# Seven-place expert ring: the down weights of two places loaded in three partition pieces instead of one

## The chip, the cores and the metric

One core of one Trainium2 chip runs the whole kernel. The metric is device time in microseconds (us) of that core. A profiled execution gives, beside its own time, a span from the first to the last instruction and a trace of engines and DMA packets. The engines are PE (matrix products), DVE (vector), ACT (scalar functions), POOL (GpSimd) and SP (which here issues the large DMAs). Sixteen DMA engines carry every transfer.

## The reference

One layer of a streaming encoder block on 256 tokens of width 1024, all in float32:

```python
h = rms_norm(x, norm_mix_gain)
proj = h @ w_in                       # q/k/v, gates, beta, decay: 5640 columns
y_a = diff_attention(...)             # 4 heads
y_b = gated_delta_net(...)            # 4 heads, chunks of 64
merged = sigmoid(m_gate_a) * (y_a @ w_branch_attn) + sigmoid(m_gate_b) * (y_b @ w_branch_gdn)
x = x + merged @ w_out
h2 = rms_norm(x, norm_ffn_gain)
x = x + hier_moe(h2, ...)             # 32 experts: 1024 -> 256 (gate, up) -> 1024 (down), 2 per token
out = rms_norm(x, norm_final_gain)
```

The change touches only how the down weights of the 32 experts (256 x 1024 float32 each, 1 MB) come from HBM to SBUF.

## The kernel before

The first 280 us are the projection, the two mixers, the output projection and the routing. The rest is the mixture of experts. Its 32 experts are visited in order, one unit of 32 token rows each (four units form a group). For every unit PE gathers the tokens of a group (line 1152), multiplies by gate and up weights (`hidden`, line 1194), turns the activation (line 1203), multiplies by the down weights (`down`, line 1239) and, once for every four units, scatters the result into the output (`scatter`, line 1249). `rolling` (line 1253) interleaves the steps: the gate and up product of unit u+1 stands ahead of the down product of unit u. The last units have forms of their own, `down_half` (line 1206) and `scatter_half` (line 1219).

Every expert needs three weights of 1 MB: gate, up and down. They live in seven places ("slots") of SBUF, of 24 KB per partition each; an eighth place holds gate and up alone, for expert 7. Expert e has its down weights in place e % 7 (`place`, line 60). A 1 MB weight is laid over 128 partitions, 8 KB of consecutive bytes in each.

All of these loads go out from SP, in program order, on one queue. `load_expert` (line 310) issues the first loads: experts 0 to 2 between the chunks of `w_in` in the first 50 us, expert 7's gate and up, and experts 3 to 6 between 234 and 266 us. From 280 us on, SP runs through the reloads: in step i it issues gate and up of expert 8+i (line 387, after a wait on `gateup_used`) and then down of expert 7+i into place i % 7 (line 392, after a wait on `experts_used`). The two waits say that PE and DVE are through with what the place held. The steps i = 0 to 22 are of this form, the first seven written out, the next fourteen in a hardware loop over two rounds of seven, the rest written out. Then come the missing columns of gate and up of expert 31 (line 412; six eighths of them were fetched early), down of expert 30, the down weights of expert 31 in two halves (line 418) and the final gain row (line 422).

A load adds 16 to its semaphore `down{slot}` when it has landed, and PE waits ahead of `down` until it stands at 16 times the number of loads that the place has had (lines 1209 and 1232).

```python
def reload_down(e, slot, used):
    sp.wait_ge(s["experts_used"], used)
    sp.dma_start(c.down_flat[slot], down_d[:, e, :].rearrange("p a f -> p (a f)")).then_inc(s[f"down{slot}"], 16)
```

Of the kernel before, what the change touches and what calls it, by code (L numbers as in the profile page):

```python
# [22 lines left out]
P = 128  # L23
# [17 lines left out]
SLOTS = 7  # L41
# [3 lines left out]
EXP_F = 3 * D * HID // P  # L45

EARLY = (4, 2)
BIG = 1e30
LAMBDA_INIT = 0.2

# [231 lines left out]
def sync_program(sp, c, io):  # L282

    s = c.s
# [11 lines left out]
    def load_chunk(i):  # L296
# [10 lines left out]
            sp.dma_start(dst[:, 0:k0, :], w_in[:, 0:k0, col:col + n]).then_inc(s["first_loaded"], 16)  # L307
        sp.dma_start(dst[:, k0:, :], w_in[:, k0:, col:col + n]).then_inc(s[f"stage_loaded{i % 2}"], 16)

    def load_expert(e):  # L310
        slot = e
        for flat, name, sem in ((c.gate_flat, "moe_w_gate", "gateup"), (c.up_flat, "moe_w_up", "gateup"),
                                (c.down_flat, "moe_w_down", "down")):
            if e == SLOTS and name == "moe_w_down":
                break
            k = 2 if name == "moe_w_down" else KD
            if e == SLOTS - 2:
                sp.wait_ge(s["mix_out"], 2)
            if e == SLOTS - 1:
                sp.wait_ge(s["mix_out"], 4)  # L320
            sp.dma_start(flat[slot], io[name][0, e].rearrange("(p k) f -> p (k f)", k=k)).then_inc(s[f"{sem}{slot}"], 16)

    load_chunk(0)
    load_chunk(1)
    load_expert(0)

    def row(dst, src, sem):
# [13 lines left out]
    for j in range(1, OWN):  # L341
        load_expert(j)
        load_chunk(2 + j)
    load_chunk(5)
    load_expert(SLOTS)
    for i in range(6, NCH):
        load_chunk(i)

    for j, name in enumerate(("w_branch_attn", "w_branch_gdn")):
        i = NCH + j  # L350
# [3 lines left out]
    for j in range(2):  # L354
        i = NCH + 2 + j
# [12 lines left out]
    def load_early(part, at, k0):  # L368

        for g, name in enumerate(("moe_w_gate", "moe_w_up")):  # L370
            sp.dma_start(at[:, g, :], io[name][0, EXPERTS - 1].rearrange("(p k) f -> p (k f)", k=KD)[:, k0 * HID:(k0 + part) * HID])\
                .then_inc(s["early_loaded"], 16)
    sp.wait_ge(s["logits_ready"], len(PIECES))
    load_early(EARLY[0], c.early_flat[0], 0)
    sp.wait_ge(s["x1_parked"], 1)
    sp.wait_ge(s["h2_ready"], NT)
    load_early(EARLY[1], c.early_flat[1], EARLY[0])

    gate_d = io["moe_w_gate"][0].rearrange("e (p k) f -> p e (k f)", k=KD)
    up_d = io["moe_w_up"][0].rearrange("e (p k) f -> p e (k f)", k=KD)  # L380
    down_d = io["moe_w_down"][0].rearrange("e (p k) d -> p e (k d)", k=2)
# [7 lines left out]
    def reload_down(e, slot, used):  # L389

        sp.wait_ge(s["experts_used"], used)
        sp.dma_start(c.down_flat[slot], down_d[:, e, :].rearrange("p a f -> p (a f)")).then_inc(s[f"down{slot}"], 16)

    def one(e):
        return slice(e, e + 1)
# [1 line left out]
    def reload_both(e, j, used, first=False):  # L397
        reload_gateup(e(1), j, used if first else used + 1)
        reload_down(e(0), j, used)
# [8 lines left out]

    e, i, had = EXPERTS - 1, loads - 1, sum(EARLY) * HID
    sp.wait_ge(s["gateup_used"], i + 2)  # L410
    for flat, src in ((c.gate_flat, gate_d), (c.up_flat, up_d)):
        sp.dma_start(flat[i % SLOTS][:, had:], src[:, one(e), had:].rearrange("p a f -> p (a f)")).then_inc(s[f"gateup{i % SLOTS}"], 16)
    reload_down(one(e - 1), i % SLOTS, i + 1)

    sp.wait_ge(s["experts_used"], e - SLOTS + 1)
# [356 lines left out]
def down_out(c, i, q):  # L772

    return c.ps[ROWS * q:ROWS * (q + 1), 2 + i % 2, 0:256]
# [7 lines left out]
def need(eng, sem, value, first):  # L782

    if not first or value > 0:
        eng.wait_ge(sem, value)
# [17 lines left out]
def tensor_program(pe, c, io):  # L803
    s = c.s
# [95 lines left out]
    i = CI["bdg"]  # L900
# [158 lines left out]
    for n in range(4):  # L1059
        j, half = n // 2, n % 2  # L1060
        i = NCH + j
# [99 lines left out]
    def windows(nwin):  # L1161
# [8 lines left out]
        def weights(slot, k, early):  # L1170

            if early and k < EARLY[0]:
                return c.early_w[0][:, :, k, :]
            if early and k < sum(EARLY):
                return c.early_w[1][:, :, k - EARLY[0], :]
            return c.gu_w[slot][:, :, k, :]
# [29 lines left out]
        def down_half(i, at, half):  # L1206

            slot, times = at[2:4]
            pe.wait_ge(s["last_down" if half else f"down{slot}"], 16 if half else times * 16)
            if half == 0:  # L1210
                pe.wait_ge(s["actT_ready"], EXPERTS)
                pe.wait_ge(s["out_copied"], 2 * EXPERTS - 4)
            for kk in range(2):
                for q in (2 * half, 2 * half + 1):
                    last = pe.matmul(down_out(c, i, q), c.actT[i % 2][:, kk * ROWS:(kk + 1) * ROWS], c.down_w[slot][:, kk, 256 * q:256 * (q + 1)],
                                     start=(kk == 0), stop=(kk == 1))
            last.then_inc(s["down_ready"], 1)
# [10 lines left out]
        def down(unit, i, at, fresh, first, last_expert=False):  # L1228

            slot, times = at[2:4]  # L1230
            if fresh:
                pe.wait_ge(s[f"down{slot}"], times * 16)
                if last_expert:
                    pe.wait_ge(s["last_down"], 16)
            pe.wait_ge(s["actT_ready"], unit + 1)
            need(pe, s["out_copied"], unit * 2 - 2, first)
            for kk in range(2):
                for q in range(4):
                    last = pe.matmul(down_out(c, i, q), c.actT[i % 2][:, kk * ROWS:(kk + 1) * ROWS], c.down_w[slot][:, kk, 256 * q:256 * (q + 1)],  # L1239
                                     start=(kk == 0), stop=(kk == 1))  # L1240
            last.then_inc(s["down_ready"], 1)
# [44 lines left out]
        def alone(grp, at, first, experts=()):  # L1286

            if not first:
                gather(grp)
            turn_weighted(grp, 1)  # L1290
            fresh = [i == 0 or at[i] != at[i - 1] for i in range(GROUP)]
            hidden(grp, 0, at[0], fresh[0], first)
            for i in range(GROUP):
                if i == 0:
                    pe.wait_ge(s["Se_ready"], grp + 1)
                if i < GROUP - 1:
                    hidden(grp, i + 1, at[i + 1], fresh[i + 1], first)
                turn_act(grp * GROUP + i, i)
                down(grp * GROUP + i, i, at[i], fresh[i], first, EXPERTS - 1 in experts[i:i + 1])
            scatter(grp)  # L1300
# [73 lines left out]
def vector_program(v, c, io):  # L1374
# [3 lines left out]
    def chain(ins):  # L1378
        n[0] += 1
        ins.then_inc(s["dve_chain"], 1)  # L1380

    def settle():
        v.wait_ge(s["dve_chain"], n[0])
# [7 lines left out]
    def side(name):  # L1391
        v.wait_ge(s["side_ready"], SI[name] + 1)
        return c.side[side_pair(name)]
# [235 lines left out]
    def maxima(qt):  # L1629

        nk = P * (qt + 1)
        for m in range(2):
            ps = side(f"s{qt}{m}").rearrange("p (h k) -> p h k", h=H)
            chain(v.memset(ps[0:CHUNK, :, nk - CHUNK:nk], -BIG))
            settle()
# [306 lines left out]
def route(v, c, chain, settle):  # L1942
# [15 lines left out]
    def over(ap, n):  # L1958
        return ap.rearrange("p (t a) -> p t a", a=1).to_broadcast([P, NT, n])

    def link(ins):
        chain(ins)
        settle()
# [16 lines left out]
    link(v.tensor_tensor(group, cand, over(c.first, GROUPS), ALU.is_equal))  # L1980
    link(v.tensor_scalar(outside, group, 1.0, BIG, ALU.subtract, ALU.mult))
    link(v.tensor_tensor(inside.rearrange("p t (g e) -> p t g e", g=GROUPS), lg[:, :, GROUPS:].rearrange("p t (g e) -> p t g e", g=GROUPS),
# [41 lines left out]
def build(nc, io):  # L2024
    with ExitStack() as ctx:
        c = lay_out(nc, ctx)

        c.A_stored = nc.dram_tensor("stored_A", (2 * H * (P * P + P),), F32, kind="Internal").ap()
        c.inverses_stored = nc.dram_tensor("stored_inverses", (2, 2 * H, P, BLOCK), F32, kind="Internal").ap()
        block = ctx.enter_context(nc.Block())  # L2030

        @block.sync
        def _(sp):
            sync_program(sp, c, io)

        @block.gpsimd
        def _(pool):
            gpsimd_program(pool, c, io)

        @block.scalar  # L2040
        def _(act):
            scalar_program(act, c, io)

        @block.tensor
        def _(pe):
            tensor_program(pe, c, io)

        @block.vector
        def _(v):
            vector_program(v, c, io)  # L2050
# [24 lines left out]
```

## Time and profile before

| | |
|---|---|
| median of 3 runs | 481.01 us (480.9 to 481.35) |
| profiled execution, its time | 480.55 us |
| its span | 478.8 us |
| PE busy | 443.7 us (93%) |
| DVE busy | 206.1 us (43%) |
| ACT busy | 123.5 us (26%) |
| bytes moved by DMA | 137.13 MB, 286 GB/s over the span |
| share of the span in the chain that ended last | PE 78%, DMA 12%, DVE 4% |

Some 1.75 us of the profiled execution lie outside its span. Busy shares are averages over stages with different limits: PE is busy at 93% in all, and has waits on DMA only in the last 80 us. In the views below, "DMA share" is the mean busy share of the 16 DMA engines in a stretch, and can read a little over 1 because packets of one engine overlap by some nanoseconds. PEclk is the granted clock of TensorE, 1.00 for full speed.

### The profile page before, as it was taken

What the parts mean: (1) busy time and instruction counts of PE and PEld (TensorE: products, weight loads), DVE (VectorE), ACT (ScalarE), POOL (GpSimd) and SP (SyncE); (2) the same over time, 40 slices, a digit from 0 to 9 for tenths busy, and PEclk for the clock granted to TensorE, in tenths of its full rate; (3) what the DMA queues carried; (4) which work ended last, traced back from release to release, by engine and by line L of the source; (5) the groups of instructions that cost most, each with busy time, mean ns of one, the idle gap of its engine ahead of it and who ended that gap; (6) DMA issues with size and microseconds to landing.
All of it is one profiled execution on the core that took longest, in us unless ns stands there. A gap on an engine that the chain in (4) does not pass through costs nothing.

```text
span 478.8 us, 10293 instructions
## 1 busy us (share of the span) xinstructions
PE 443.7 (93%) x4337; PEld 336.4 (70%) x4337; DVE 206.1 (43%) x588; ACT 123.5 (26%) x311; POOL 11.8 (2%) x36
## 2 busy tenths in 40 slices
PE   8999999999999999999999798998989896698793
PEld 7885698875988799888645487575767664566451
DVE  1366287997344451711310645343434342413324
ACT  5001523001032230420012643232323322212234
POOL 6011000000000000000000000000000000000000
PEclk9999999999999999999999999999999998978798
DMA  8969947717504050444399869999999999999972
GB/s 314 399 198 349 410 155 235 287 41 213 177 7 171 0 177 2 175 177 175 127 421 414 330 258 422 417 417 422 418 420 417 420 420 419 420 419 422 418 284 93
DMA packets 38178, 137.13 MB, mean 286 GB/s; under 512 B 8561, under 2 KB 9905, under 8 KB 26225
## 3 DMA queue, kind: packets, MB, share of 16 engines
q1 hardware_dynamic: 33776, 135.22, 71.4%
q10 hardware_dynamic: 4352, 1.21, 1.2%
q8 instruction: 36, 0.59, 0.5%
q14 instruction: 14, 0.11, 0.1%
HBM read 134.59 MB, written 1.84 MB: 285 GB/s over the span
## 4 chain that ended last, share of the span: by engine, by line
PE 78%; DMA 12%; DVE 4%; issue 2%; ACT 2%; ACTq 0%; DVEq 0%
PE ps L868 30%; PE ps L1194 11%; DMA arena<-in_moe_w_up 6%; PE ps L1090 6%; PE ps L1075 6%; DMA ring<-in_moe_w_up 6%; PE ps L1152 5%; PE ps L1239 4%; PE ps L1249 4%; PE ps L886 3%; PE ps L1203 2%; DMA cst_in<-in_norm_ffn_gain 1%; PE ps L1021 1%; PE ps L983 1%; PE ps L906 1%
## 5 line engine op out<-in xcount | busy, mean ns | idle before, releaser
L868 PE MATMUL ps<-arena 128*128 128x256 f32 (+1 forms) x640 | 155.9, 401 | 0.2 <-ACT arena L516 0.2
L868 PEld LDWEIGHTS ps<-arena 128*128 128x128 f32 x640 | 119.9, 190 | 29.0 <-issue 14.6
L1194 PE MATMUL ps<-arena 128*32 128x128 f32 x1072 | 40.8, 292 | 9.8 <-DMA arena<-in_moe_w_up 6.0
L1194 PEld LDWEIGHTS ps<-arena 128*32 128x32 f32 x1072 | 31.3, 114 | 17.8 <-issue 7.8
L1194 PE MATMUL ps<-ring,arena 128*32 128x128 f32 x912 | 34.4, 293 | 8.4 <-DMA ring<-in_moe_w_up 7.1
L681 ACT ACTIVATE gains<-ps 32x256 f32<-32x256 f32 x62 | 23.3, 376 | 56.9 <-PE ps L1239 56.6
L1194 PEld LDWEIGHTS ps<-ring,arena 128*32 128x32 f32 x912 | 26.6, 114 | 14.8 <-DMA ring<-in_moe_w_up 8.6
L1849 DVE TENSOR_TENSOR masks<-ps,masks 128x64 f32<-128x64 f32 x32 | 7.2, 224 | 62.9 <-ACT masks L662 62.7
L1152 PEld LDWEIGHTS ps<-masks,arena 128*128 128x128 f32 x256 | 29.4, 193 | 3.4 <-issue 3.4
L1152 PE MATMUL ps<-masks,arena 128*128 128x128 f32 x256 | 30.8, 279 | 0.8 <-DVE masks L1786 0.8
L1864 DVE COPY arena<-ps 32x256 f32<-32x256 f32 x62 | 25.8, 416 | 11.5 <-PE ps L1239 10.2
L1090 PE MATMUL ps<-arena 128*128 128x512 f32 x64 | 28.3, 595 | 0.0
L1075 PE MATMUL ps<-arena 128*128 128x256 f32 x128 | 28.0, 379 | 0.0
L1075 PEld LDWEIGHTS ps<-arena 128*128 128x128 f32 x128 | 24.2, 190 | 3.3
L1090 PEld LDWEIGHTS ps<-arena 128*128 128x128 f32 x64 | 11.9, 190 | 13.4 <-issue 13.4
L568 ACT ACTIVATE arena<-ps 128x1024 f32<-128x1024 f32 x7 | 7.2, 1023 | 51.9 <-PE ps L868 32.4
L668 ACT ACTIVATE masks<-ps 64x64 f32<-64x64 f32 x32 | 6.9, 217 | 41.4 <-PE ps L1203 41.4
L1239 PE MATMUL ps<-arena,masks 128*32 128x256 f32 x256 | 17.0, 382 | 0.0
L1203 PE MATMUL ps<-masks 128*64 128x128 f32 x128 | 15.1, 316 | 1.2 <-DVE masks L1851 1.0
L1249 PE MATMUL ps<-arena,rw 128*128 128x512 f32 x28 | 16.2, 660 | 0.0
L1239 PE MATMUL ps<-ring,masks 128*32 128x256 f32 x240 | 16.0, 382 | 0.0
L1834 DVE TENSOR_TENSOR arena<-ps,small 128x512 f32<-128x512 f32 x8 | 5.5, 692 | 23.4 <-PE ps L1152 23.4
(271 smaller groups left out, 465.7 us busy)
## 6 DMA issues: line engine op xcount, KB each, us to landing
arena<-in_w_in SPq DMA_DIRECT2D x9, 2048.0 KB, 9.1
arena<-in_moe_w_gate SPq DMA_DIRECT2D x16, 1024.0 KB, 23.4
arena<-in_moe_w_up SPq DMA_DIRECT2D x16, 1024.0 KB, 24.8
arena<-in_moe_w_down SPq DMA_DIRECT2D x16, 1024.0 KB, 23.6
ring<-in_moe_w_down SPq DMA_DIRECT2D x15, 1024.0 KB, 23.7
ring<-in_moe_w_gate SPq DMA_DIRECT2D x14, 1024.0 KB, 20.3
ring<-in_moe_w_up SPq DMA_DIRECT2D x14, 1024.0 KB, 22.6
arena<-in_w_out SPq DMA_DIRECT2D x2, 2048.0 KB, 8.2
```

The costliest lines, as they stand in the source:

```text
L568: act.activation(dst, c.pair[i % 2], func).then_inc(s[sem], 1)
L681: last = act.activation(stacked(c, i, q), down_out(c, i, q), ACT.Copy)
L868: last = pe.matmul(out, lhs, rhs, start=(k == 0 and (i > 0 or part % 2 == 0)), stop=(k == KD - 1), skip_group_check=(i == 0))
L886: last = pe.matmul(blk(ps, i), lhs(t, h), rhs(t, h), start=True, stop=True)
L1075: last = pe.matmul(blk(branch_out(c, half), b, TOK), w[:, k, (4 * half + b) * P:(4 * half + b + 1) * P], yT[:, k, :], start=(k == 0), stop ...
L1090: last = pe.matmul(c.ps[:, 4 + 2 * t + half, :], mg, w[:, k, :], start=(k == 0), stop=(k == KD - 1))
L1152: last = pe.matmul(gather_out(c, k), c.h2[:, t, k, :], c.oh[:, t, :], start=(t == 0), stop=(t == NT - 1))
L1194: last = pe.matmul(c.ps[ROWS * q:ROWS * (q + 1), i % 2, 0:P], c.Hg[:, k, ROWS * i:ROWS * (i + 1)], w[:, :, start:start + 127:2], start=(k ...
L1203: last = pe.matmul(c.ps[64 * half:64 * half + 64, i % 2, 0:P], c.act[i % 2][:, 0:64], c.ident, start=True, stop=True)
L1239: last = pe.matmul(down_out(c, i, q), c.actT[i % 2][:, kk * ROWS:(kk + 1) * ROWS], c.down_w[slot][:, kk, 256 * q:256 * (q + 1)], start=(kk ...
L1249: last = pe.matmul(y_out(c, half, t), c.S_e[:, t * P:(t + 1) * P], c.Y[half], start=False, stop=False, skip_group_check=True)
L1864: last = v.tensor_copy(stacked(c, i, q), down_out(c, i, q))
```

## The change

The places 2 and 5 are named in `PARTED`. Wherever a whole down weight is loaded into one of them, in `load_expert` and in `reload_down`, three DMAs are issued instead of one: partitions 0 to 111, partitions 112 to 119, and partitions 120 to 127. Each adds 16 to the same semaphore, so for these two places PE waits for 48 per load and not for 16. The bytes, the order of the loads, the waits of SP and all other places are as they were. The two half loads of expert 31 go to place 3 and are not touched. Nine loads are of the new form: experts 2 and 5 at first, and as reloads the experts 9, 12, 16, 19, 23, 26 and 30.

```diff
+PARTED = (2, 5)
+DOWN_SIGNALS = [48 if i in PARTED else 16 for i in range(SLOTS)]
...
+    def down_parts(slot):
+        return [slice(0, P - 16), slice(P - 16, P - 8), slice(P - 8, P)] if slot in PARTED else [slice(0, P)]
...
-            sp.dma_start(flat[slot], io[name][0, e].rearrange("(p k) f -> p (k f)", k=k)).then_inc(s[f"{sem}{slot}"], 16)
+            src = io[name][0, e].rearrange("(p k) f -> p (k f)", k=k)
+            for rows in down_parts(slot) if name == "moe_w_down" else [slice(0, P)]:
+                sp.dma_start(flat[slot][rows], src[rows]).then_inc(s[f"{sem}{slot}"], 16)
...
     def reload_down(e, slot, used):
 
         sp.wait_ge(s["experts_used"], used)
-        sp.dma_start(c.down_flat[slot], down_d[:, e, :].rearrange("p a f -> p (a f)")).then_inc(s[f"down{slot}"], 16)
+        for rows in down_parts(slot):
+            sp.dma_start(c.down_flat[slot][rows], down_d[rows, e, :].rearrange("p a f -> p (a f)")).then_inc(s[f"down{slot}"], 16)
...
-            pe.wait_ge(s["last_down" if half else f"down{slot}"], 16 if half else times * 16)
+            pe.wait_ge(s["last_down" if half else f"down{slot}"], 16 if half else times * DOWN_SIGNALS[slot])
...
-                pe.wait_ge(s[f"down{slot}"], times * 16)
+                pe.wait_ge(s[f"down{slot}"], times * DOWN_SIGNALS[slot])
```

## Rows read from the trace of the kernel before

**Rows 1.** The page's chain that ended last, shares of the span.

```profile
PE 78%; DMA 12%; DVE 4%; issue 2%; ACT 2%; ACTq 0%; DVEq 0%
```

**Rows 2.** Waits of PE, 280 to 479 us: total us, times, longest.

```profile
PE ps L1194 <- DMA ring<-in_moe_w_up: 7.1, 2, 3.8
PE ps L1194 <- DMA arena<-in_moe_w_up: 6.0, 2, 3.9
```

**Rows 3.** Timeline of PE, 395 to 455 us: start, us, what, [idle before <-releaser].

```profile
402.70 1.36 PE L1194 MATMUL ps<-ring,arena 128*32 128x128 f32 x32 [3.84 <-DMA ring<-in_moe_w_up]
...
418.63 1.94 PE L1194 MATMUL ps<-arena 128*32 128x128 f32 x32 [3.92 <-DMA arena<-in_moe_w_up]
...
448.89 1.94 PE L1194 MATMUL ps<-ring,arena 128*32 128x128 f32 x32 [3.26 <-DMA ring<-in_moe_w_up]
```

**Rows 4.** Windows: stretch, busy us of the engines, PEclk, DMA share, GB/s.

```profile
core 0: us, PE busy (x) PEld busy (x) DVE busy (x) ACT busy (x) POOL busy (x), PEclk, DMA share, GB/s
281.00:449.00 168.00, 148.30 (x2610) 106.34 (x2614) 63.78 (x203) 47.50 (x168) 0.00 (x0) 0.96 1.01 417
```

**Rows 5.** DMA queues, 281 to 449 us: packets, MB, share of 16 engines.

```profile
q1 hardware_dynamic: 9563, 69.69, 100.2%
q8 instruction: 21, 0.34, 0.8%
q14 instruction: 5, 0.04, 0.1%
```

**Rows 6.** Windows over the end of the last loads.

```profile
460.00:461.00 1.00, 1.00 (x37) 0.94 (x37) 0.00 (x0) 0.43 (x2) 0.00 (x0) 1.00 0.97 385
...
461.00:466.00 5.00, 3.93 (x100) 2.66 (x94) 1.72 (x6) 2.78 (x7) 0.00 (x0) 1.00 0.48 188
...
466.00:467.00 1.00, 1.00 (x20) 0.51 (x23) 0.00 (x0) 0.67 (x4) 0.00 (x0) 1.00 0.00 0
```

**Rows 7.** The last issues, by line: durations in ns, starts; time to landing.

```profile
L422 SPq DMA_DIRECT2D arena<-in_norm_final_gain x1: 4289/4289/4289, 449.2 to 449.2; - x1
...
DMA to landing us min/median/max: 17.2/17.2/17.2
```

**Rows 8.** The two half loads of expert 31, by line.

```profile
L418 SPq DMA_DIRECT2D arena<-in_moe_w_down x2: 2157/3401/4645, 442.3 to 444.5; - x2
...
DMA to landing us min/median/max: 20.6/21.1/21.6
```

**Rows 9.** Timeline of SP: first and last reloads of place 2.

```profile
295.84 0.33 SPq L392 DMA_DIRECT2D ring<-in_moe_w_down  x1
...
436.02 6.28 SPq L392 DMA_DIRECT2D ring<-in_moe_w_down  x1
```

**Rows 10.** Store from 32 partitions: its line, and the queues from 107 to 109 us.

```profile
L574 ACTq DMA_DIRECT2D stored_inverses<-arena x2: 312/378/444, 106.7 to 107.0; - x2
...
q10 hardware_dynamic: 96, 0.26, 57.2%
```

**Rows 11.** Store of the output from 128 partitions: the queues from 474.5 to 478.5 us.

```profile
q1 hardware_dynamic: 288, 1.05, 65.5%
```

**Rows 12.** Timeline of PE at the end.

```profile
465.89 1.07 PE L1239 MATMUL ps<-ring,masks 128*32 128x256 f32 x16
466.79 1.09 PE L1215 MATMUL ps<-arena,masks 128*32 128x256 f32 x16
```

## The prediction

> **What bounds the kernel now.** I read the chain that ended last first. It is 78% PE and 12% DMA [rows 1], so a change to loads can matter only where the DMA part lies. The list of PE's waits from 280 us on has four on a DMA, 7.1 + 6.0 = 13.1 us in all, and every one is the product with gate and up weights waiting for an up weight [rows 2]. The timeline shows where: three of the four stand at 402.70, 418.63 and 448.89 us [rows 3], the fourth lies between the last two. So PE has slack until some 400 us and is paced by the loads from there to 448.89. After that no wait on a DMA follows, and the remaining 29.9 us of the 478.8 us span are a fixed tail. **The end is the landing of that last awaited weight plus 29.9 us.**
>
> Which weight is it? Counting the expert products back from the end (31 at 462.5, 30 at 458.7), the one at 448.89 belongs to expert 29, and what it awaits is the up load of step i = 21. Before it stand 21 steps of three loads and one gate, 65 loads with itself. The windows show the stream without a hole: DMA share 1.01 and 417 GB/s over 168 us [rows 4]. At 16 engines and one packet of 8 KB per partition, the queue's row gives the price of a packet: 100.2% of 16 x 168 us over some 8,500 weight packets (69.69 MB / 8 KB) is 0.317 us [rows 5]. A load of 128 partitions is 8 packets per engine, 2.53 us.
>
> A load has landed when the last of the 16 engines is through. How far are they apart? At the end of the stream the share is 0.97 in the us before 461, 0.48 on average over 461 to 466, and 0 after [rows 6]; the gain row, last in the queue, lands at 449.2 + 17.2 = 466.4 [rows 7]. So the first engines are idle from about 461 and the last works to 466.4: some 5 us between the first and the last. In those 5.4 us the mean engine works 5 x 0.48 = 2.4 us, so it is through 3.0 us ahead of the last. One cause is visible: 21 instruction packets of 16 KB, at 0.8% x 16 x 168 us = 21.5 us or 1.0 us each [rows 5], which an engine carries beside its share of weights. Spread evenly they would be 1.3 us for each engine; a gap of 5 us needs some engines to carry most of them. No view names these engines.
>
> **The change, part by part.**
>
> *SP's issues.* Two more DMAs in each of 9 loads. A reload of place 2 takes SP 0.33 us early in the stream, and 6.28 us late in it, when SP is held up because the queue ahead is full [rows 9]. Loads issued 17 to 22 us ahead of their landing [rows 7, 8] hide an issue of 0.4 us. Cost 0; without this cover 2 x 0.4 x 6 = 5 us. The first loads of places 2 and 5 (about 44 and 250 us) lie where PE waits for no weight. Also 0. What is queued behind each on SP are the next gate and up, with the same cover.
>
> *PE's waits.* The same waits on another number. 0.
>
> *The 112-partition piece.* One packet less for each engine if 16 engines still carry it, seven each: -0.317 us per load on all of them.
>
> *The two pieces of 8 partitions.* The trace has no such load in the stream. One packet is one partition, so at most eight engines carry a piece; if nothing holds them up it costs each of them one packet, 0.317 us. At the other end the eight packets go one after the other, 8 x 0.317 = 2.5 us. What is nearest in the trace? A store of 2 x 128 KB that has 32 partitions at the SBUF end: 64 packets of 4 KB in 57.2% of 16 x 2 us, 0.286 us each [rows 10]. The output's store has packets of the same 4 KB from 128 partitions: 65.5% of 16 x 4 us over 256 of them, 0.164 us each [rows 11]. With four times fewer partitions under the same 16 engines a packet takes 1.74 times as long. So a few partitions can't be served at the rate of the engines: 32 gave 16 x 4,096 B / 0.286 us = 229 GB/s, 7.2 GB/s per partition. At this rate 8 partitions give 57 GB/s, and a piece of 64 KB takes 1.14 us. I take this value; the ends 0.317 and 2.5 us stay for the range.
>
> The Trainium skill states the rule behind it: in "SBUF — State Buffer", Door 1, four neighbouring partitions share one of 16 ports, and the rate of a DMA goes by the ports that its partitions reach. By its map each piece here reaches two ports and would take about 1.2 us, an estimate from its 27.2 GB/s per port; the trace agrees on the 32 partitions. The page "DMA: Bandwidth & Descriptors", on how many engines a DMA uses, would put 8 partitions on the eight lowest-numbered engines, both pieces on the same eight; no row here shows it.
>
> *The sum.* An engine that carries both pieces spends 7 x 0.317 + 2 x 1.14 = 4.50 us on a parted load instead of 2.53, +1.97 us. Ahead of the awaited up weight lie the steps with i % 7 = 2 or 5: 2, 5, 9, 12, 16, 19, six loads. That is +11.8 us. The engines are up to 5 us apart, so they don't always meet at the same partitions; I take nine tenths, +10.6 us. Against it stands the lead: an average engine is 3.0 us ahead of the one that ends a load now, and this much is swallowed. Net **+7.6 us** on the landing at 448.89, and, since only the fixed tail follows, on the end. The other eight engines gain 6 x 0.317 = 1.9 us, but are no longer last.
>
> The seventh parted reload (expert 30) comes after that landing. It adds 2.0 us to the loads behind it: the halves of expert 31, which land at about 463.9 and 465.1 [rows 8], would be at 465.9 and 467.1 in the old timing, while their first product starts at 466.79 [rows 12] and the second half is used about 0.5 us on. This is just covered; 0, at worst 0.5.
>
> Against its own time: 480.55 + 7.6 = 488.2 us for an execution like the profiled one; the median of the runs is 0.46 us above that, so 481.0 + 7.6 = **488.6 us**.
>
> **The rivals.**
>
> *A. The pieces don't queue, and they go to the engines with the lead.* Then each parted load moves one packet from the eight late engines to the eight early ones: 1.9 us less on the one side, 1.9 us more on the other, by the sixth. Even engines would be worth 3.0 us [rows 6]; the late ones can come down by 1.9 at most, and the latest of the early ones comes up by as much and takes over before that. I put it at -1.3 us: 479.7 us. For it: instruction packets are real, and 5 us apart is what they would leave on few engines. Against: rows 10. It decides the sign where a piece costs these engines less than about 0.43 us: twelve times the excess over 0.317 must stay under 1.3 us.
>
> *B. No queueing, but the eight are the late ones.* +6 x 0.317 = +1.9 us, 482.9 us. It hangs on which engines fetch instructions, which no view tells.
>
> *C. A little queueing that eats the gain of A*, within 0.9 us: 481.0 us. It needs a piece at 0.35 to 0.5 us.
>
> *D. The 112-partition piece queues too.* Seven partitions per engine no longer fall the way eight do; if two engines meet throughout at the price of rows 10, the piece costs 0.74 x 2.2 = 1.6 us more on every engine, 9.8 us over six loads, so about +17 us: 498 us. Against: the 128-partition loads and the 32-partition store both run at what their partitions allow, and 112 lies near 128.
>
> *E. The loads aren't what is awaited.* If PE had slack, nothing would move. Against it stand 13.1 us of waits [rows 2].
>
> **How the numbers follow.** The forecast has 0.58; its own range is from half of the queueing (5.9 - 3.0 = +2.9) to all of it with no lead and slower neighbours (+15): 484 to 496 us. A 0.17, B 0.09, C and E 0.10, D 0.06. A whole change of 0.2% (0.96 us) is what can be told from none here. Faster: A, and a little of C, 0.19. Same: 0.08. Slower: 0.73. The range reaches down to A, whose place is only just below the old time, and up to the top of the forecast: 479.5 to 496.5; D and the far ends are left out.
>
> **What would show it.** DMA packets: 16 more semaphore writes for each of 9 loads, 38,178 + 144. Right: the four waits on up weights grow from 13.1 us to 20 or more, the first of them comes before 400 us; the GB/s between 281 and 449 falls from 417 to about 395, with DMA share still near 1.0 as packets get longer; the gain row lands some 8 to 10 us later; the tail behind the last wait stays near 29.9 us. For A: the waits shrink by about 1.3 us, the share in the last 5 us of loading rises above 0.48. For D: GB/s falls under 380. The prediction is wrong if a small piece costs its engines no more than an ordinary packet, or if these engines had more lead than 3 us.

## The result, and the profile after

The changed kernel takes 522.93 us (median of 4, 521.49 to 527.3) against 481.18 us for the kernel before on the same chip (480.9 to 482.99): ratio 1.089, 95% interval 1.0858 to 1.0923. It is 41.8 us slower (by the medians), where the forecast said 7.6 and its range ended at 496.5. The sign was right, the size and the step that makes it were not.

Two lines of the page after: shares of the chain that ended last, and GB/s in 40 slices of the 520.9 us span.

```profile
PE 70%; DMA 20%; DVE 4%; issue 3%; ACT 2%; SPq 0%; ACTq 0%; DVEq 0%
...
GB/s 317 370 202 406 305 104 322 163 75 289 0 163 0 162 33 135 158 161 316 421 318 289 420 309 417 293 416 396 287 411 256 415 353 287 386 255 405 287 139 89
```

The DMA part has grown from 12% [rows 1] to 20%. From slice 24 on, the rate is no longer flat: between stretches at 386 to 417 it drops seven times, to 309 at first and to 255 to 293 later. Each drop is a parted load (one that is issued in pieces). The queues and the windows of the changed kernel give their price (same columns as [rows 4]):

```profile
281.00:449.00 168.00, 134.59 (x2324) 95.96 (x2312) 56.23 (x181) 40.94 (x145) 0.00 (x0) 0.92 1.00 353
```

```profile
300.00:318.00 18.00, 14.86 (x268) 10.20 (x261) 5.89 (x21) 4.24 (x15) 0.00 (x0) 1.00 1.01 337
324.00:342.00 18.00, 14.30 (x256) 9.38 (x249) 5.54 (x20) 4.24 (x15) 0.00 (x0) 0.95 1.01 325
360.00:378.00 18.00, 14.98 (x290) 11.42 (x283) 7.72 (x26) 5.60 (x20) 0.00 (x0) 1.00 1.02 305
390.00:408.00 18.00, 9.71 (x129) 6.81 (x127) 4.76 (x15) 3.30 (x11) 0.00 (x0) 0.81 1.02 294
420.00:444.00 24.00, 15.87 (x272) 11.24 (x260) 7.54 (x25) 5.49 (x21) 0.00 (x0) 0.86 1.01 313
450.00:474.00 24.00, 16.37 (x212) 10.35 (x205) 4.60 (x16) 3.05 (x11) 0.00 (x0) 0.73 1.01 303
474.00:486.00 12.00, 8.11 (x148) 6.26 (x151) 4.52 (x13) 3.30 (x11) 0.00 (x0) 0.90 1.02 415
486.00:498.00 12.00, 8.76 (x78) 4.47 (x70) 1.70 (x5) 1.41 (x5) 0.00 (x0) 0.78 1.00 230
498.00:504.00 6.00, 5.85 (x84) 3.79 (x84) 0.44 (x2) 0.66 (x3) 0.00 (x0) 0.50 0.52 161
504.00:510.00 6.00, 5.00 (x108) 3.14 (x104) 2.04 (x6) 4.00 (x12) 0.00 (x0) 0.99 0.08 28
```

How to read it: the engines are "busy" all the time (share 1.00 to 1.02) while they move 300 GB/s and not 417. They don't lack work; their packets take longer. And not the packets of the parted load alone: from 486 to 498 us 12 x 230 = 2.8 MB are moved at the low rate, and a parted load is 1.05 MB. With 417 GB/s as the undisturbed rate, the first window misses (417 - 337) x 18 / 417 = 3.5 us; the next five miss 4.0, 4.8, 5.3, 6.0 and 6.6. That is 30.1 us in six parted loads, and each costs more than the one before. The seventh (expert 30) takes another 5.4 us out of 486 to 498. In the last line 8% of the engines' time is left: about one engine is still at it.

PE's waits from 280 us on, as [rows 2] (the lines of the kernel lie nine further down now: L1203 is `hidden`, L1194 before):

```profile
PE ps L1203 <- DMA arena<-in_moe_w_up: 21.9, 5, 7.4
PE ps L1203 <- DMA ring<-in_moe_w_up: 14.4, 4, 5.4
PE ps L1203 <- issue: 9.1, 4, 3.7
```

Four waits on an up weight have become nine, 13.1 us have become 36.3. The last of them in the timeline, as [rows 3], and the same product (expert 30) in the kernel before:

```profile
484.88 1.94 PE L1203 MATMUL ps<-ring,arena 128*32 128x128 f32 x32 [3.89 <-DMA ring<-in_moe_w_up]
...
498.15 1.94 PE L1203 MATMUL ps<-ring,arena 128*32 128x128 f32 x32 [3.39 <-DMA ring<-in_moe_w_up]
```

```profile
458.66 1.10 PE L1194 MATMUL ps<-ring,arena 128*32 128x128 f32 x32
```

The last awaited weight is now expert 30's, one expert later than before: 39.5 us at this product. Behind it the tail is 520.9 - 498.15 = 22.75 us where it was 478.8 - 458.66 = 20.1; PE runs it at first at half clock (PEclk 0.50 from 498 to 504, 1.94 us for 32 products instead of 1.10). 39.5 + 2.6 is the span's 42.1 us. Of the 39.5, the windows show 30.1 + 5.4, which is what the mean engine loses up to 498 us; the other 4.0 I put down to the last engine falling further behind the mean. The landings in the trace show that it does: each of the 16 engines reports its share of a load. The down weights of expert 29, right behind the awaited weight, landed from 453.5 to 458.8 us in the kernel before, the last 2.7 us behind the mean of the sixteen. In the changed kernel they landed from 484.2 to 501.2, the last 11.0 behind the mean. So this load's mean landing is 34.1 us later, its last 42.4. (In e10 below, the same kernel again, it landed from 483.7 to 494.5.)

Of the signs that the prediction named for its own forecast, the waits came (36.3 us, 20 or more forecast); the rate and the gain row moved the forecast way, but several times as far: 353 GB/s (about 395 forecast), and the row 43.5 us later (8 to 10). The packets came as counted, 144 more on the loads' queue. The sign of rival D, under 380 GB/s, came too.

### The profile page after: what moved, and what is told of

Read it like the earlier page. It is cut to its first block, busy times and chain, and to the rows that moved or that the text cites. A ratio compares the mean times of both kernels' runs of the same rounds, so it can differ in the third digit from the quotient of the medians.

```text
span 520.9 us, 10327 instructions
## 1 busy us (share of the span) xinstructions
PE 458.0 (88%) x4337; PEld 344.8 (66%) x4337; DVE 205.9 (40%) x588; ACT 123.5 (24%) x311; POOL 11.8 (2%) x36
## 4 chain that ended last, share of the span: by engine, by line
PE 70%; DMA 20%; DVE 4%; issue 3%; ACT 2%; SPq 0%; ACTq 0%; DVEq 0%
PE ps L877 28%; DMA arena<-in_moe_w_up 13%; PE ps L1203 9%; DMA ring<-in_moe_w_up 7%; PE ps L1099 5%; PE ps L1084 5%; PE ps L1161 4%; PE ps L1248 4%; PE ps L1258 3%; PE ps L895 3%; PE ps L1212 2%; DMA cst_in<-in_norm_ffn_gain 1%; PE ps L1030 1%; PE ps L992 1%; PE ps L915 1%
## 5 line engine op out<-in xcount | busy, mean ns | idle before, releaser
L1203 PE MATMUL ps<-arena 128*32 128x128 f32 x1072 | 44.7, 313 | 26.6 <-DMA arena<-in_moe_w_up 21.9
L1203 PEld LDWEIGHTS ps<-arena 128*32 128x32 f32 x1072 | 33.7, 122 | 36.1 <-DMA arena<-in_moe_w_up 24.5
L1203 PE MATMUL ps<-ring,arena 128*32 128x128 f32 x912 | 36.6, 307 | 15.7 <-DMA ring<-in_moe_w_up 14.4
L1203 PEld LDWEIGHTS ps<-ring,arena 128*32 128x32 f32 x912 | 28.0, 120 | 22.9 <-DMA ring<-in_moe_w_up 16.4
L1161 PEld LDWEIGHTS ps<-masks,arena 128*128 128x128 f32 x256 | 30.7, 200 | 3.4 <-issue 3.4
L1161 PE MATMUL ps<-masks,arena 128*128 128x128 f32 x256 | 32.2, 286 | 0.8 <-DVE masks L1795 0.8
L1212 PE MATMUL ps<-masks 128*64 128x128 f32 x128 | 16.3, 331 | 2.8 <-issue 1.8
L1248 PE MATMUL ps<-ring,masks 128*32 128x256 f32 x240 | 17.1, 404 | 0.4 <-DMA ring<-in_moe_w_down 0.4
```

The costliest lines, as they stand in the source:

```text
L1161: last = pe.matmul(gather_out(c, k), c.h2[:, t, k, :], c.oh[:, t, :], start=(t == 0), stop=(t == NT - 1))
L1203: last = pe.matmul(c.ps[ROWS * q:ROWS * (q + 1), i % 2, 0:P], c.Hg[:, k, ROWS * i:ROWS * (i + 1)], w[:, :, start:start + 127:2], start=(k ...
L1212: last = pe.matmul(c.ps[64 * half:64 * half + 64, i % 2, 0:P], c.act[i % 2][:, 0:64], c.ident, start=True, stop=True)
```

## The experiments

Theories, as the expectations name them: **S**, the forecast (only the two pieces of eight partitions queue); **N**, each further DMA costs; **Q**, what counts is how the partitions of a DMA lie, and the 112-partition piece has most of the loss.

**e1, 112 and 16 partitions.**

```diff
-        return [slice(0, P - 16), slice(P - 16, P - 8), slice(P - 8, P)] if slot in PARTED else [slice(0, P)]
+        return [slice(0, P - 16), slice(P - 16, P)] if slot in PARTED else [slice(0, P)]
```

(Here and in e3, e8, e9 and e11 the count that PE waits for, 48, follows the number of DMAs.)

> Places 2 and 5 get their down weights as 112 and 16 partitions, two DMAs. Three theories. S (the forecast): only the two eight-partition pieces queue, so with them gone most of the loss of 42 us goes; 16 neighbouring partitions at the 7.2 GB/s per partition of the 32-partition store take 0.57 us instead of 0.32, so 482 to 486 us. Q: the 112-partition piece itself is slow, because seven partitions per engine no longer match how SBUF is reached, and engines meet at the same partitions; then 505 to 525 us. N: each further DMA costs by its number; one more instead of two, about half the loss, 500 to 503 us.

520.03 us, ratio 1.083 (1.0716 to 1.0944). Nearly all of the loss stays without a piece of eight, as Q has it. S falls.

**e2, three DMAs of all partitions, cut by columns.**

```diff
-            for rows in down_parts(slot) if name == "moe_w_down" else [slice(0, P)]:
-                sp.dma_start(flat[slot][rows], src[rows]).then_inc(s[f"{sem}{slot}"], 16)
+            for cols in down_parts(slot) if name == "moe_w_down" else [slice(0, 2048)]:
+                sp.dma_start(flat[slot][:, cols], src[:, cols]).then_inc(s[f"{sem}{slot}"], 16)
```

(and the same in `reload_down`; the columns are 0:1792, 1792:1920, 1920:2048.)

> Places 2 and 5 get their down weights in three DMAs of all 128 partitions, cut by columns: 7 KB, 0.5 KB and 0.5 KB of each partition. N (the number of DMAs costs): as the changed kernel, 515 to 525 us. S and Q (what partitions a DMA has is what costs): within 2 us of the kernel before, 480 to 483 us; the rate of the loads between 281 and 449 us stays at 410 GB/s or more.

482.01 us, ratio 1.0021 (0.9978 to 1.0064), no difference that can be told. N falls as the cause. The rate was a little under the expected 410:

```profile
281.00:449.00 168.00, 150.82 (x2658) 109.01 (x2658) 63.45 (x202) 47.63 (x166) 0.00 (x0) 0.95 0.99 406
```

**e3, two halves of 64 partitions**: `[slice(0, 64), slice(64, P)]`.

> Places 2 and 5 get their down weights as two DMAs of 64 partitions. S: no small piece, so 480 to 483 us. N: about half the loss, 500 to 503 us. Q: the sixteen engines have four partitions each of one half of SBUF, two engines wherever one was; each such load takes up to 2.5 us more, six of them ahead of the last awaited weight: 490 to 500 us.

Two runs, 517.96 and 527.51 us, too far apart for a ratio; 37.2 and 46.8 us above the kernel before on the same chip (480.74). No piece is small, no count is odd, each engine has four whole partitions, and the loss is all there. I expected 9 to 19 us by Q: the direction held, the size didn't.

**e4, the small pieces over every second partition**: `[slice(0, P - 16), slice(P - 16, P, 2), slice(P - 15, P, 2)]`.

> As the changed kernel, but the two eight-partition pieces take every second partition of the last sixteen instead of eight neighbours each, so that two engines and not four meet at each group of four partitions. N: no difference, 521 to 525 us. S: the small pieces are the whole loss and get cheaper by up to half: 500 to 508 us. Q with the 112-partition piece as the larger part: a few us less than the changed kernel, 512 to 521 us.

527.55 us, ratio 1.0987 (1.0893 to 1.108). Not cheaper. All three expectations were missed on the low side, the one of N the least (e2 has ruled N out). e5 below has eight partitions spread wider still (every fourth) at half the price of eight neighbours. If the small pieces made the loss, spreading them should have saved some of it; what is left is the 112-partition piece.

**e5, the loads by themselves.** Behind the stored output of the kernel before, batches of loads of 8 KB rows, each waited out:

```diff
+    def batch(*loads):
+        for n, (rows, width) in enumerate(loads):
...
+            sp.dma_start(dst, src).then_inc(s["out_stored"], 16)
+        done[0] += 16 * len(loads)
+        sp.wait_ge(s["out_stored"], done[0])
+    full, w = slice(0, P), 2048
+    eight = slice(64, 96, 4)
+    for rows in (full, slice(0, 112), slice(0, 64), slice(112, P), slice(112, 120), eight):
+        batch(*[(rows, w)] * 4)
...
```

> The kernel before, with loads of 8 KB rows behind the stored output, by themselves, in batches that SP waits out. Its time has no meaning beside the others; the lengths of the batches have. Four loads each of 128, 112, 64, 16 neighbouring, 8 neighbouring and 8 every-fourth partitions; then five of 128; then 128, 128, 64+64, 128, 128; then the same with 112+16; then the last row sets again (five of 128; with 64+64) behind eight loads of 24 KB rows that only one half of the engines carries, so that this half is some 4 us late. Q (each group of four neighbouring partitions has one entrance, shared with the group 32 further, and engines are dealt neighbouring blocks): 4 x 128 takes 10 us and a fixed 2; 64 takes as long as 128, half the rate; 8 neighbours 1.2 us each, 8 every-fourth 0.3 to 0.4 us each; 128,128,64+64,128,128 takes 2.5 us more than five of 128, and more than that behind the late half, 4 us or more. If the partitions don't matter: 64 takes half of 128, 8 neighbours as 8 spread, and no set of the same bytes is longer than another.

Windows of e5 from the first issue of a batch to the first issue of the next (same columns; the length is the second number, some 1.4 us of it are not transfer: the packets of the first batch span 11.0 us of its 12.33). In order: four of 128, of 112, of 64, of 16, of 8 neighbours, of 8 every fourth; five of 128; with 64+64 in the middle; with 112+16; then, each from the first weight load on, behind the eight 24 KB-row loads, five of 128 and the set with 64+64.

```profile
478.50:490.83 12.33, 0.00 (x0) 0.00 (x0) 0.00 (x0) 0.00 (x0) 0.00 (x0) 0.50 0.86 341
490.83:506.91 16.08, 0.00 (x0) 0.00 (x0) 0.00 (x0) 0.00 (x0) 0.00 (x0) 0.50 0.87 228
506.91:519.39 12.48, 0.00 (x0) 0.00 (x0) 0.00 (x0) 0.00 (x0) 0.00 (x0) 0.50 0.77 168
519.39:525.61 6.22, 0.00 (x0) 0.00 (x0) 0.00 (x0) 0.00 (x0) 0.00 (x0) 0.50 0.58 84
525.61:531.87 6.26, 0.00 (x0) 0.00 (x0) 0.00 (x0) 0.00 (x0) 0.00 (x0) 0.50 0.28 42
531.87:536.51 4.64, 0.00 (x0) 0.00 (x0) 0.00 (x0) 0.00 (x0) 0.00 (x0) 0.50 0.18 57
536.51:551.26 14.75, 0.00 (x0) 0.00 (x0) 0.00 (x0) 0.00 (x0) 0.00 (x0) 0.50 0.88 355
551.26:569.45 18.19, 0.00 (x0) 0.00 (x0) 0.00 (x0) 0.00 (x0) 0.00 (x0) 0.50 0.87 288
569.45:586.28 16.83, 0.00 (x0) 0.00 (x0) 0.00 (x0) 0.00 (x0) 0.00 (x0) 0.50 0.89 312
592.07:612.99 20.92, 0.00 (x0) 0.00 (x0) 0.00 (x0) 0.00 (x0) 0.00 (x0) 0.50 0.85 293
618.35:644.60 26.25, 0.00 (x0) 0.00 (x0) 0.00 (x0) 0.00 (x0) 0.00 (x0) 0.50 0.87 231
```

Three readings. Four loads of 64 neighbours take as long as four of 128 (12.48 and 12.33 us): half the bytes, half the rate. Four of 112 take 3.75 us *longer* than four of 128, 0.94 us each with an eighth less to move; against a proportional 7/8 of the transfer, (16.08 - 1.4) / 4 - 7/8 x (12.33 - 1.4) / 4 = +1.3 us. And a parted load amid whole ones costs 18.19 - 14.75 = 3.4 us as halves and 2.1 us as 112+16 when the engines start in step, but 26.25 - 20.92 = 5.3 us as halves when half of the engines are late (the last window ends with the span; up to the last landings of the two sets the difference is 5.0 us). Each set ran once.

The share of the engines' time, divided by the packets, gives the price of one packet of 8 KB: 0.33 us in whole loads (0.86 x 16 x 12.33 / 512), 0.50 in loads of 112, 0.60 in loads of 64 neighbours, 0.90 in those of 16, 0.88 with eight neighbours and 0.42 with eight spread. (The batches of eight differ by 6.26 - 4.64 us, 0.4 us per load, but SP had the fourth of the spread ones out only 2.1 us behind the first, so their time is partly that of the issues.) So my price for a small piece, 1.14 us, was of the right kind and somewhat high.

The Trainium skill, in "SBUF — State Buffer", Door 1, says that 64 neighbouring partitions reach no more ports than 32, half of all 16. Four of 64 at the pace of four of 128 agree with it. By this rule alone a parted load as halves would take 2.5 us more, an estimate (half the rate for a load that takes 2.53 us whole); e5 shows 3.4 to 5.3.

**e6, the changed form at place 2 alone**: `PARTED = (2,)`.

> The changed form at place 2 alone: three of the six parted loads ahead of the last awaited weight (steps 2, 9, 16). If each parted load costs by itself, and more the further the engines have drifted apart (3.5 us at step 2, some 5 us at steps 9 and 16, plus what the last engine falls behind): about half of 42 us or a little less, 497 to 504 us. If the loss comes from one stall or from all six together, it is far from half: under 490 or over 515 us.

503.33 us (500.8 and 505.85), ratio 1.0445 (1.0317 to 1.0572): 22 us, half of the loss from half of the parted loads ahead of the last awaited weight. It comes load by load. The three drops of the rate ahead of the end, the changed kernel's first, third and fifth:

```profile
300.00:318.00 18.00, 14.04 (x213) 9.19 (x202) 4.60 (x16) 3.22 (x12) 0.00 (x0) 0.84 1.01 330
357.00:375.00 18.00, 14.73 (x260) 11.07 (x248) 7.42 (x24) 4.94 (x17) 0.00 (x0) 0.91 1.02 307
414.00:432.00 18.00, 11.81 (x176) 8.61 (x168) 4.96 (x15) 3.96 (x14) 0.00 (x0) 0.88 1.01 286
```

They miss 3.8, 4.7 and 5.7 us, against 3.5, 4.8 and 6.0 in the changed kernel. With half as many parted loads ahead of it, a load at the same place costs nearly the same: what makes the later ones dearer is the place in the stream, not the parted loads before.

**e7, which engines carry a piece of eight.** Three extra loads late in the stream of the kernel before:

```diff
+        sp.dma_start(c.extra[64:96:4, 16 * n:16 * n + 16], io["moe_w_gate"][0, n].rearrange("(p k) f -> p (k f)", k=KD)[0:8, 0:16]).then_inc(s["lambda_loaded"], 16)
```

> The kernel before with three extra loads of 8 partitions x 64 bytes late in the stream of reloads, which carry nothing that is used. They do next to nothing to the time (480 to 483 us). Their landings show which of the sixteen engines carry an eight-partition load. If these are the engines that carry no instruction packets: they land with the early half of the sixteen landings of the load ahead of them, up to 2 us after its first. If they are the ones with the instruction packets: with the late half, 3 to 5 us after the first.

481.26 us. The landings, one per engine, of a whole load of 128 partitions, and of the probe right behind it (times of the trace's own clock, in us):

```
load, 16 engines: 459.08 459.09 459.20 459.28 459.73 459.79 460.68 461.17
                  462.15 462.23 462.46 463.70 463.71 463.78 463.91 464.33
probe, 8 engines: 459.30 459.38 459.46 460.05 460.86 461.36 462.36 462.68
```

By these times a probe comes some 0.2 us behind its engine's load. So an eight-partition load runs on eight engines, and here they are six of the early half and two of the middle; in the third probe one of the eight is as late as the late group (475.52, against 475.62 for that load's last). Neither expectation is met cleanly: the eight are mostly the early engines, but not all. If the pieces of the changed kernel go to the same eight, which no run shows, they could not have evened the engines out even without queueing, since one of the eight ends up among the late ones.

The landings of the kernel before also show how the engines drift apart. The first and the last landing of the seven loads that the change parts (experts 9, 12, 16, 19, 23, 26, 30) lie 1.7, 2.2, 3.3, 3.8, 4.6, 4.9 and 5.3 us apart there.

**e8, the even and the odd partitions**: `[slice(0, P, 2), slice(1, P, 2)]`.

> Places 2 and 5 get their down weights as two DMAs of 64 partitions again, but as the even and the odd partitions. Q, by capacity alone: each of the two reaches all of SBUF's entrances, so the load costs nothing by itself, 480 to 490 us. Q, by order: a block of four such rows still walks over entrances that another engine walks over at the same time, two engines everywhere: as the halves, 510 to 525 us. If it is the split into halves of SBUF that matters, 480 to 490 us too.

481.3 us, ratio 0.9987 (0.9967 to 1.0008). As many partitions per DMA as in e3, as many DMAs, and no loss:

```profile
281.00:449.00 168.00, 150.11 (x2670) 107.41 (x2662) 65.61 (x210) 47.73 (x169) 0.00 (x0) 0.96 1.00 412
```

against the halves (the longer of e3's two runs; the shorter has the loss too):

```profile
281.00:449.00 168.00, 136.37 (x2330) 97.48 (x2329) 57.34 (x183) 42.46 (x147) 0.00 (x0) 0.92 0.99 341
```

The pair e3 and e8 is the cleanest of all: what counts is which partitions a DMA has together, not how many. One thing it can't separate: partition p always gets the p-th 8 KB of the weight, so neighbouring partitions are also neighbouring bytes in HBM. Whether the loss arises at the SBUF end or at the HBM end is not shown; a run with the rows of the weight shuffled over the partitions would tell.

**e9, every fourth partition, four DMAs**: `[slice(i, P, 4) for i in range(4)]`.

> Places 2 and 5 get their down weights as four DMAs of 32 partitions, every fourth partition each, so that every DMA has one partition in each group of four neighbours. Q (what counts is whether the partitions of a DMA lie evenly over all of SBUF's groups): within 2 us of the kernel before, 480 to 483 us, though no DMA has 128 partitions and there are four where there was one. N (number of DMAs) and any theory by which only 128 or 64 partitions are dealt out well: 500 us or more.

481.59 us, ratio 1.0016 (0.9995 to 1.0037). Four DMAs of 32 partitions, free as well.

**e10 and e11, the changed kernel again beside 112 and 16.**

> The changed kernel again, beside the next one on the same chip, to price the two eight-partition pieces against one of sixteen. S in what is left of it (small pieces cost something beside the large one): 2 to 8 us above the next kernel. Q with nearly all of the loss in the 112-partition piece: within 2 us of it.

> Places 2 and 5 as 112 and 16 partitions again, now with three rounds: 518 to 522 us by Q, and within 2 us of the kernel with two eight-partition pieces; 2 to 8 us below it by what is left of S.

521.0 us, ratio 1.0837 (1.0799 to 1.0876), and 518.81 us, ratio 1.0807 (1.0747 to 1.0867). The intervals overlap: two pieces of eight cost at most a few us beside one of sixteen, 2.2 us by the medians, of 40. That lies on the border of the two expectations and decides between neither; either way it is a small part.

**e12, expert 30's reload alone in the new form.**

```diff
-    reload_down(one(e - 1), i % SLOTS, i + 1)
+    reload_down(one(e - 1), i % SLOTS, i + 1, (slice(0, P - 16), slice(P - 16, P - 8), slice(P - 8, P)))
...
```

(`reload_down` takes the parts as an argument here, and PE waits for 112 signals on this one load: four whole loads and three DMAs.)

> The kernel before, with the new form (112, 8, 8 partitions) for the reload of expert 30 alone, the last of the seven and behind every up weight that PE waits for. By the order of landing, as the forecast had it, this one is covered: 0 to 1 us, 480.5 to 482 us. If engines that are ahead and already in the 112-partition piece slow the engines that are still in earlier loads, and everything behind it comes 4 to 6 us later for the last engine, the 2 to 3 us of cover at the end are used up: 2 to 6 us more, 483 to 487 us.

486.53 us, ratio 1.0125 (1.0078 to 1.0172). The load that stands behind every awaited up weight costs 4.4 us by the medians (482.1 before), 6 by the ratio. PE's timeline of e12, the last wait on an up weight and the waits behind it:

```profile
450.68 1.93 PE L1195 MATMUL ps<-ring,arena 128*32 128x128 f32 x32 [3.05 <-DMA ring<-in_moe_w_up]
...
463.82 1.07 PE L1240 MATMUL ps<-ring,masks 128*32 128x256 f32 x16 [0.82 <-issue]
...
466.28 1.58 PE L1195 MATMUL ps<-arena 128*32 128x128 f32 x48 [1.02 <-issue]
...
469.88 1.07 PE L1240 MATMUL ps<-ring,masks 128*32 128x256 f32 x16 [0.16 <-DMA ring<-in_moe_w_down]
...
472.22 1.06 PE L1216 MATMUL ps<-arena,masks 128*32 128x256 f32 x8 [0.23 <-DMA arena<-in_moe_w_down]
```

The first is as before (3.05 us beside 3.26 [rows 3]); it stands 1.8 us later, but ahead of the parted load's drop of the rate (from some 455 us on), so I put that down to scatter between runs. The tail behind it is 484.2 - 450.68 = 33.5 us where it was 29.9. The waits at 463.82 and 466.28 ahead of the products of experts 29 and 31 have no releaser in the view; the weights of both are issued *ahead of* the parted load. Their last landings in the trace are 463.7 and 466.2 us, right ahead of the two products. The load of expert 29 landed from 455.6 to 463.7 here and from 453.5 to 458.8 in the kernel before: its first engine is 2.1 us later, its last 4.9. This is a whole load, issued ahead of the only parted one of this run, and its last engines are slowed: the clearest sign that engines already in the parted load hold up those that aren't there yet.

## Why the prediction was wrong

*What bounds the kernel*: right. The stream sets the end; PE's waits grew with it, and the tail moved little.

*SP's issues and the count in PE's waits at 0*: right; e2 and e9 have as many or more DMAs and signals and show it.

*The 112-partition piece, -0.317 us on every engine*: **this is the first step that failed.** I costed it by its number of packets, a row of whole loads at 0.317 us each, and took for granted that sixteen engines with seven packets run as sixteen with eight. e5 has it 0.94 us *longer* than a whole load, seven packets of 0.50 us each. That is 1.3 us more than I gave it, 7.7 us over six loads. Rival D had the mechanism, "seven partitions per engine no longer fall the way eight do", priced 1.6 us a load and about 17 us in all, and I gave it 0.06 with the argument that 112 lies near 128. Nearness is no argument: e8 and e9 split a load in two and in four for nothing, e3 in two for 40 us.

*The two pieces of eight, 2 x 1.14 us*: the kind is right (e5: a packet of 0.88 us with eight neighbours, 0.42 with eight spread), but in the stream two of them cost hardly more than one of sixteen (e10, e11: 2.2 us in all) and spreading them saves nothing (e4).

*The price of a load is local, and the lead of 3.0 us swallows part of it*: the second failure, and the larger in us. With the right price of the 112-partition piece the forecast's own sum would have said some 15 us; the other 26 or 27 are here. The sum charges the engines that carry a piece, and those alone. But the packets of a parted load slow those of other engines that are still, or already, in whole loads (the 2.8 MB at 230 GB/s, and the load of expert 29 in e12). In step a parted load costs 2.1 us as 112+16 (e5), at the first place in the stream 3.5 and at the sixth 6.6. My reading of the rise: the engines drift apart on the way, by 1.7 us at the first and 5.3 us at the seventh in the kernel before, and the further apart they are, the longer some engine is in a parted load while others are beside it. e5 shows the direction with halves, 3.4 against 5.3 us, and e6 that it is the place that counts. No lead was swallowed either: the last engine fell further behind, from 2.7 to 11.0 us behind the mean.

*The seventh parted load at 0*: wrong for the same reason. e12 measures it at 4 to 6 us. In the changed kernel early engines were in it while late ones still carried expert 30's up weight, the awaited one: by the landings the first engine was through with its share of the 112 partitions at 489.9 us, the last one with its share of the awaited weight at 498.1.

*Rival A* (a gain): the mechanism that denied it is the one above; e7 adds that the eight engines of such a load were not the eight that lead.

*What stays open*: the map from partitions to engines. Q by order, with two engines meeting at every row, would have made e8 as slow as e3; it isn't, so a DMA whose partitions lie evenly runs without loss though no run tells which engine takes which. The side, SBUF or HBM, as said under e8. And the half rate of 64 neighbours explains 2.5 us of a load as halves, not the rest of the 3.4 to 5.3.

## What to carry to other kernels

Cut by columns, or by every second or fourth partition, a load of this kernel cost nothing even in a full stream; cut into runs of neighbouring partitions (112+8+8, 112+16, 64+64) it took the whole stream down to some 200 to 300 GB/s of 417, for longer than its own bytes need. Don't price a transfer by bytes or packets alone when its partitions are other than those of the rows that the price is from: measure four of it alone, as e5 does, before putting it on a path that is bound by loads. And where all engines are busy and the rate is low, look at how long a packet takes, not at how many there are. What waits is the last engine, so look at how far apart the engines land, too.

## What was not expected of the hardware

Engines at a busy share of 1.00 moved 230 GB/s from 486 to 498 us in the changed kernel, where 417 is usual: the share says nothing about progress. PE's waits without a seen releaser grew too, from a longest of 1.5 us in the kernel before to 3.1 us ahead of 314.6 and 3.7 us ahead of 339.2, at the ends of the first two drops of the rate. The view counts instruction packets among those of the sixteen engines [rows 5]; they may be late with the others, which no run tested.
